# Differential attention on one core: the projection ahead of the transposes of the mixed map in each slot

## The reference, cut to what matters

```
q, k, v = split(h @ w_qkv)                  # 8 heads: two queries and keys of 64, one value of 128
q, k = rope(first 16 of 64), rest unchanged
sc = einsum(q, k) * 64 ** -0.5              # two maps of 1024 x 1024 per head
p = softmax(sc)
a = p[0] - lam * p[1]                       # the mixed map
o = einsum(a, v)                            # then an RMSNorm per head, then @ w_o
```

## Time and profile before

| | before |
|---|---|
| median of 3 runs | 2977.08 us |
| profiled execution, device time | 2978.38 us |
| its span in the trace | 2976.6 us |
| TensorE busy over the span | 2776.4 us (93%) |
| VectorE busy | 1827.4 us (61%) |
| ScalarE busy | 1369.5 us (46%) |
| GpSimd busy | 1388.5 us (47%) |
| slots of the differential attention | about 1561 to 2135 us of the span |

### The profile page before, as it was taken

One profiled execution on the slowest core, in us unless ns is written; L12 is line 12 of the kernel. 1 busy time (PEld: TensorE's weight loads), 2 busy tenths in 40 slices (PEclk: granted clock), 3 DMA queues, 4 the chain that ended last, 5 costly groups with the idle time before them and its releaser, 6 DMA issues. The chain is left out here.

```text
span 2976.6 us, 40948 instructions
## 1 busy us (share of the span) xinstructions
PE 2776.4 (93%) x13932; PEld 2336.2 (78%) x13932; DVE 1827.4 (61%) x2528; ACT 1369.5 (46%) x2098; POOL 1388.5 (47%) x1065
## 2 busy tenths in 40 slices
PE   6799999998979999999979999999796999999997
PEld 5688888887758888788857888887685788887886
DVE  6377777775465445555568887888636454455556
ACT  4466666765244444421236565655423444443211
POOL 3244343343277777653433333332225777775441
PEclk9999999999989999999989999999898999999998
DMA  3000000002212122343120000000331222225221
GB/s 111 27 10 10 9 9 9 9 19 92 106 43 77 75 81 85 136 154 113 42 94 29 29 29 29 28 29 8 118 117 49 81 78 76 83 85 219 85 85 57
DMA packets 53089, 195.20 MB, mean 66 GB/s; under 512 B 6400, under 2 KB 6656, under 8 KB 52608
## 3 DMA queue, kind: packets, MB, share of 16 engines
q1 hardware_dynamic: 52992, 193.95, 17.7%
HBM read 148.84 MB, written 45.09 MB: 65 GB/s over the span
## 5 line engine op out<-in xcount | busy, mean ns | idle before, releaser
L1089 PE MATMUL ffn_ps<-ffn_b_hi,weights_hi 128*128 128x512 f32 x704 | 278.2, 395 | 43.0 <-ACT ffn_parts L866 29.1
L338 POOL TENSOR_TENSOR weights_lo<-weights_raw,weights_hi 128x1024 fp32r<-128x1024 f32 (+1 forms) x64 | 142.8, 2231 | 342.7 <-ACT weights_hi L333 342.7
L1091 PE MATMUL ffn_ps<-ffn_b_hi,weights_lo 128*128 128x512 f32 x704 | 277.1, 394 | 0.0
L1090 PE MATMUL ffn_ps<-ffn_b_lo,weights_hi 128*128 128x512 f32 x704 | 276.9, 393 | 0.0
L942 POOL TENSOR_TENSOR ffn_local_lo<-ffn_sums,ffn_local_hi 128x512 fp32r<-128x512 f32 x126 | 169.2, 1345 | 107.7 <-ACT ffn_local_hi L822 107.7
L991 POOL TENSOR_TENSOR ffn_y_lo<-ffn_y_raw,ffn_y_hi 128x1024 fp32r<-128x1024 f32 x44 | 108.9, 2496 | 229.5 <-ACT ffn_y_hi L905 229.5
L1944 ACT ACTIVATE dif_p<-dif_s,dif_neg_max 128x1024 f32<-128x1024 f32 x128 | 142.2, 1113 | 136.3 <-DVE dif_neg_max L2126 125.2
L822 ACT ACTIVATE ffn_local_hi<-ffn_sums 128x512 fp32r<-128x512 f32 x126 | 79.2, 632 | 258.5 <-PE ffn_ps L1091 158.5
L1089 PE MATMUL ffn_ps<-ffn_b_hi,ffn_local_hi 128*128 128x512 f32 x504 | 196.2, 389 | 0.0
L1090 PE MATMUL ffn_ps<-ffn_b_lo,ffn_local_hi 128*128 128x512 f32 x504 | 196.1, 389 | 0.0
L1091 PE MATMUL ffn_ps<-ffn_b_hi,ffn_local_lo 128*128 128x512 f32 x504 | 196.1, 389 | 0.0
(11 more groups left out here) (291 smaller groups left out, 8557.2 us busy)
## 6 DMA issues: line engine op xcount, KB each, us to landing
weights_raw<-in_up SPq DMA_DIRECT2D x44, 512.0 KB, 4.2
ffn_up_raw<-in_up SPq DMA_DIRECT2D x44, 512.0 KB, 3.9
ffn_products<-ffn_conv SPq DMA_DIRECT2D x44, 512.0 KB, 2.6
ffn_y_raw<-ffn_products SPq DMA_DIRECT2D x44, 512.0 KB, 4.1
ffn_down_raw<-in_down SPq DMA_DIRECT2D x24, 512.0 KB, 6.2
weights_raw<-in_diff_qkv SPq DMA_DIRECT2D x24, 512.0 KB, 3.6
weights_raw<-in_down SPq DMA_DIRECT2D x20, 512.0 KB, 5.9
x_spill<-x_in SPq DMA_DIRECT2D x16, 512.0 KB, 2.8
```

The costliest lines, as they stand in the source:

```text
L338: pool.tensor_tensor(w.lo[:], w.raw[:], w.hi[:].bitcast(F32), ALU.subtract).then_inc(w.lo_done, 1)
L1089: pe.matmul(out, hi, x_hi, start=start, stop=False, skip_group_check=True)
L1090: pe.matmul(out, hi, x_lo, start=False, stop=False, skip_group_check=True)
L1091: return pe.matmul(out, lo, x_hi, start=False, stop=stop, skip_group_check=True)
```

## The change

In TensorE's slot the transposes of the mixed map become a function of their own, `turn_maps`. It is called where it stood in slot 3 and in the four slots behind the last head; in every other slot it is called behind the projection, and in slot 4 ahead of `sum_head`. The code of the other engines is unchanged.

```diff
+            def turn_maps(t, n, first, scores):
+                if not (first and t == 0) and (scores or t == 0):
+                    pe.wait_ge(mixed, n)
+                    for half in range(2):
+                        need(pe, pt_lo_done, 2 * n + (half - 3))
+                        for k in range(4):
+                            k0 = (4 * half + k) * P
+                            mm = pe.transpose(turn_ps[half][:, k * P:(k + 1) * P],
+                                              p0[(t - 1) % 2][:, k0:k0 + P], cst[:, C_IDENT:C_IDENT + P])
+                        mm.then_inc(turned, 1)
+
...
                 if t % 2 == 1 and not (first and t < LAG_V):
                     values(h, t)
-                if not (first and t == 0) and (scores or t == 0):
-                    pe.wait_ge(mixed, n)
...
-                        mm.then_inc(turned, 1)
+                if t == 3 or not scores:
+                    turn_maps(t, n, first, scores)
                 if not scores:
                     return
                 if t == 0:
...
                     if t in (5, 6):
                         project(h + 1, V0 if t == 5 else V1, wkv, 2 * h + 3)
+                if t != 3:
+                    turn_maps(t, n, first, scores)
                 if t == 4 and not first:
                     sum_head(h)
```

## The result

The changed kernel takes 3056.57 us (median of 4 runs, 3051.61 to 3057.45) against 2977.45 us before in the same comparison: ratio 1.026, 95% interval 1.0247 to 1.0272. It is slower, as forecast, but by 79 us instead of 50, and lies above the range (3004 to 3043). The span of the profiled execution is 3055.7 us.

A forecast was written before the change was run, and what follows sets the result against it. TensorE was taken to bound the kernel. Heads 1 to 6 (42.3 us), head 0 (4.75) and head 7 (0.5) gave 47.5 us; with 3 us for the clock, +50.5, a median of 3027 us, range 3004 to 3043.

The forecast's parts named there:

- What bounds the stage, and what is moved: TensorE bounds head 4, busy 69.94 of 73.00 us; 42 of 64 slots get their 8 transposes behind a projection.
- Term A: Slots 1 to 4: VectorE's late row of work delays projection Q0 2.91 us, plus 0.79 for slot 4's transposes: +3.7 a head.
- The contention: Rotation of Q1 beside GpSimd's weight subtraction: its first product stays at 2.33 us; at 0.68 A would be 1.65 smaller.
- Term B: Slot 4: sums of squares newly wait 1.84 us on ScalarE's square, slot 5's 1.73 us wait goes: +0.1 us a head.
- the wait of slot 5: TensorE's 1.73 us wait ahead of slot 5's value product, on VectorE's sums, goes; if it stayed, B would be +1.8.
- Term C: Slots 5 to 0: S of slot 0 waits 3.5 us for q's low part, 0.25 before: +3.25 us a head.
- T of slot 5: Start of Term C's chain: from slot 5's transposes to the end of the exponentials takes 8.96 us.
- the 0.6 us from T to ScalarE: Estimated time from the transposes' start to ScalarE's first high part, bounds 0.4 and 1.0; it enters every term.
- Heads 0 and 7: Head 0 adds 4.75 us (A 1.5, C 3.25); head 7 adds 0.5, between 0 and 1.3.
- The clock: Granted clock falls behind Term C's wait: half of 0.9 us lost in seven places, 3 us in all.
- Rival 3: Clock falls at each new wait and for longer, 2.5 us lost seven times instead of 3 us: 3042 us, chance 0.12.
- The range: Forecast's own range 3013 to 3040 us; with part of rival 2 and the centre of Rival 3, 3004 to 3043.
- rival 2: VectorE catches up in slots 2 and 3, Term A is absorbed, only Term C is left: 3000 us, chance 0.12.

The follow-up runs named there:

- slot 1 alone: The kernel before the change with the transposes moved behind the projection in slot 1 only, all other slots as before: 3006.88 us, ratio 1.0098.
- first filled run: The changed kernel with unread identity transposes filling four TensorE waits, 28 of them ahead of S in slot 0: 3049.34 us, ratio 1.024.
- the second: The changed kernel with the same filling transposes, but those for the wait on q at the end of slot 7, 26 long: 3041.37 us, ratio 1.0215.

## Why the prediction was wrong

**What bounds the stage, and what is moved**: right. The removed waits were worth 2.7 us (those on the low parts fell from 6.1 to 4.0, that on the mix went); the moved transposes made the work behind them on the other engines late.

**Term A**: right in size and cause. T of slot 1 to P(Q0) took 23.40 us for 23.03, and slot 1 alone gives the term. The contention stayed as taken: the rotation of Q1 took 3.4 us in head 4, in other proportions (first product 0.68, sum 2.70, the latter beside the weight subtraction). The small waits inside it were there too, 0.4 on the take of K0 and 1.96 on that of K1.

**Term B**: right. The sums wait 1.68 us (forecast 1.84), the wait of slot 5 is gone. That wait was a little smaller than the 1.73 us I took off for six heads: two of the six stood in the list under "issue", at 1.2 us each.

**Term C**: right, 9.88 us for 9.77; and the step "T of slot 5" in it turned out to be a second, independent cause, which I read past when I expected something of putting slot 6 back. Of the 0.6 us from T to ScalarE, in every term, the changed kernel shows 0.69 in slot 1 of head 4.

**Heads 0 and 7**: head 0 grew from 67.2 to 74.1 us, 6.9 for a forecast of 4.75, nearly all of it idle time (4.6 to 11.1), so A was nearer its full size there than the 1.5 I took. Head 7 grew by some 3 us for 0.5; its clock went from 0.90 to 0.86, its busy time rose by 4.0 us and its idle time fell by 1.1.

**The clock**: this is the step that failed, as the prediction put it: "I take half of 0.9 in seven places, 3 us". The busy time of the same matmuls rose by 29.7 us. Two things were wrong in it. First the price: one fall cost 1.7 to 3.4 us in head 4, where I had taken 0.9 from a stretch in which TensorE had mostly been idle, and left out the 0.84 of the stretch after. Second the place: I priced only the one long wait and looked for a threshold between 3.06 and 3.44 us of idle time. At that place the clock cost 5.0 us in heads 1 to 6 and 1.7 in head 7; the other 20 of heads 1 to 6 went in slots 3 and 4, behind clusters of waits (U at 1920, U at 1925, P at 1930, sums at 1938, none over 2.2 us) and, for 15 of them, at the sums that the change put directly behind a short T and a wait. Rival 3 had the mechanism, with a chance of 0.12, but its 3042 us rest on the same seven places. The fillings show that this is a cost of its own: with most of the idle time filled by useless work the kernel took 15 us less. How much of the falls of slot 4 is due to the waits ahead and how much to the sums themselves, no run separates.

**The range**: its upper end is not the sum of its own parts. 47.5 us for the terms, 10 for the wait of slot 5 and 17 for the clock give 3052 us for the median, where the forecast's own range ended at 3040. The measured 3056.57 lies above that too.

## What to carry to other kernels

A call moved on the bounding engine makes everything late that stands behind its reader on the other in-order engines: walk those rows to the next thing the bounding engine needs, and look for more than one path, since undoing one of two gives nothing. Then price the clock for all new idle time in the neighbourhood, clusters of short waits and rows of tiny matmuls beside them too, and not only for the longest wait; here it added 60% to the waits themselves. Waits that are cheap to remove may lie on another engine: two calls swapped on VectorE gave 0.3%, where this reordering of TensorE took 2.6%.

## What the runs showed of the hardware

With slot 5 or 6 moved alone the granted clock fell at a single idle time of 3.1 us at S of slot 0 in each of heads 1 to 6 (0.63 over the next 8 us in head 4), and not in head 7 of the run with slot 6; in the fully changed kernel it fell there in heads 2, 4, 5 and 7 only, though the wait was as long in all. Before the change an idle 3.06 us in head 7 had cost nothing (1.00 over the next 6 us); with the sums taken first, and TensorE's order the same, it did (0.72). So the length of the last wait does not settle it, and which of these waits drops the clock is left open; what is shown is the sum. With useless transposes in the waits the clock of heads 1 to 6 stayed at 0.99. Behind the 16 one-column matmuls of the sums it fell with only 0.16 us idle ahead of them, in three of six heads of the first filled run and in one of the second. The Trainium skill (TensorE: Matmul & The Clock Gate, Part 1) says the clock gate follows how busy the array has been; the clusters in head 4 (0.62 over 9 us, no wait over 2.2 us) agree. The one stop that I can't explain is the 4.47 us that TensorE stood ahead of the filler at the turn of its loop, ascribed to issue; with the filler ahead of the turn 1.95 us were left of it.
